# One core, a two-layer RWKV / attention decoder with 16 experts per layer: the list of tokens per expert is made by one-hot products, the router's parameters come a stage earlier, and the router's product stands on four column groups

## What is computed

```python
def hier_moe(x, w_grp, b_grp, w_exp, b_exp, w_gate, w_up, w_down):
    grp_logits = (t @ w_grp) + b_grp                 # 512 x 4
    grp = argmax(grp_logits); p_grp = softmax(grp_logits)[grp]
    exp_logits = (t @ w_exp) + b_exp                 # 512 x 4 x 4
    sel = exp_logits of the chosen group
    top_v, top_i = lax.top_k(sel, 2); top_w = softmax(top_v)
    gate = one_hot(grp) * within(top_i, top_w) * p_grp   # 512 x 16
    for e in range(16):                              # hidden width 512
        hdn = silu(t @ w_gate[e]) * (t @ w_up[e])
        y = y + gate[:, e:e + 1] * (hdn @ w_down[e])

h = x
for layer in (0, 1):
    h = h + (rwkv7_time_mix if layer == 0 else dilated_attention)(rmsnorm(h, norm_mix_g[layer]))
    h = h + hier_moe(rmsnorm(h, norm_ffn_g[layer]), ...)
return rmsnorm(h, final_norm_g)
```

## Time and profile before

| | us |
|---|---|
| median of three runs | 1850.54 |
| lowest, highest | 1848.89, 1855.57 |
| the profiled execution, its own time | 1855.97 |
| its span in the trace | 1854.3 |
| granted TensorE clock, mean | 0.882 of full speed |
| PE, DVE, ACT, POOL busy | 1457.0, 1029.9, 821.4, 269.7 |

### The profile page before, as it was taken

One profiled execution on the slowest core, in us unless ns is written; L12 is line 12 of the kernel. 1 busy time (PEld: TensorE's weight loads), 2 busy tenths in 40 slices (PEclk: granted clock), 3 DMA queues, 4 the chain that ended last, 5 costly groups with the idle time before them and its releaser, 6 DMA issues. The chain is left out here.

```text
span 1854.3 us, 28295 instructions
## 1 busy us (share of the span) xinstructions
PE 1457.0 (79%) x11205; PEld 1099.6 (59%) x11205; DVE 1029.9 (56%) x1191; ACT 821.4 (44%) x1169; POOL 269.7 (15%) x255
## 2 busy tenths in 40 slices
PE   3899986677715837999996499999985449999991
PEld 2273864566613316788775386777774337887771
DVE  4332446444455055888884524444445438888883
ACT  2223323344410025777774333334441327777761
POOL 1000017533231021010111200000001030111101
PEclk8598995899966968999998699999976769999995
DMA  4032200011160075999995422111200549999974
GB/s 143 2 139 87 91 1 0 22 27 26 26 266 36 14 272 186 393 393 391 393 391 188 155 91 68 46 46 46 69 0 1 195 148 377 393 391 392 391 296 159
DMA packets 162389, 313.02 MB, mean 169 GB/s; under 512 B 30256, under 2 KB 31536, under 8 KB 161520
## 3 DMA queue, kind: packets, MB, share of 16 engines
q1 hardware_dynamic: 149904, 265.36, 40.3%
q0 software_dynamic: 7488, 25.24, 3.7%
q10 hardware_dynamic: 4896, 20.97, 2.8%
HBM read 282.12 MB, written 29.43 MB: 168 GB/s over the span
## 5 line engine op out<-in xcount | busy, mean ns | idle before, releaser
L1158 DVE TENSOR_TENSOR moe_wlo<-moe_raw,moe_whi 128x2048 fp32r<-128x2048 f32 x192 | 436.7, 2290 | 88.2 <-ACT moe_whi L1154 88.0
L1154 ACT ACTIVATE moe_whi<-moe_raw 128x2048 fp32r<-128x2048 f32 x192 | 363.4, 1915 | 44.0 <-DMA moe_raw<-in_moe_w_down_dram 20.8
L1165 PE MATMUL all_bank<-moe_whi,moe_xhi 128*128 128x512 f32 x512 | 206.6, 403 | 4.1 <-DVE moe_xlo L1210 4.1
L1167 PE MATMUL all_bank<-moe_whi,moe_xlo 128*128 128x512 f32 x512 | 200.7, 392 | 0.0
L1166 PE MATMUL all_bank<-moe_wlo,moe_xhi 128*128 128x512 f32 x512 | 200.3, 391 | 0.0
L1165 PEld LDWEIGHTS all_bank<-moe_whi,moe_xhi 128*128 128x128 f32 x512 | 97.0, 189 | 23.5 <-DVE moe_xlo L1210 4.9
L1167 PEld LDWEIGHTS all_bank<-moe_whi,moe_xlo 128*128 128x128 f32 x512 | 96.6, 189 | 20.9
L1166 PEld LDWEIGHTS all_bank<-moe_wlo,moe_xhi 128*128 128x128 f32 x512 | 97.1, 190 | 18.3
L1165 PE MATMUL all_bank<-moe_whi,moe_hhi 128*128 128x512 f32 x256 | 102.8, 402 | 4.4 <-issue 4.4
L1166 PE MATMUL all_bank<-moe_wlo,moe_hhi 128*128 128x512 f32 x256 | 101.4, 396 | 0.0
L1167 PE MATMUL all_bank<-moe_whi,moe_hlo 128*128 128x512 f32 x256 | 101.3, 396 | 0.0
(11 more groups left out here) (366 smaller groups left out, 2963.9 us busy)
## 6 DMA issues: line engine op xcount, KB each, us to landing
moe_raw<-in_moe_w_gate_dram SPq DMA_DIRECT2D x64, 1024.0 KB, 12.4
moe_raw<-in_moe_w_up_dram SPq DMA_DIRECT2D x64, 1024.0 KB, 13.2
moe_raw<-in_moe_w_down_dram SPq DMA_DIRECT2D x64, 1024.0 KB, 12.0
out_dram<-moe_yo ACTq DMA_DIRECT2D x32, 512.0 KB, 6.3
attn_xhat<-in_w_kv_dram SPq DMA_DIRECT2D x10, 1024.0 KB, 5.0
attn_xhat<-in_attn_w_q_dram SPq DMA_DIRECT2D x6, 1024.0 KB, 4.9
all_h<-in_rwkv_w_v_dram SPq DMA_DIRECT2D x4, 1024.0 KB, 8.2
all_h<-in_rwkv_w_k_dram SPq DMA_DIRECT2D x4, 1024.0 KB, 6.3
```

The costliest lines, as they stand in the source:

```text
L1154: nc.scalar.activation(whi[slot % SPLITS][:, :], raw[slot % 6][:, :], ACT.Copy).then_inc(m["hi_ok"], 1)
L1158: nc.vector.tensor_tensor(wlo[slot % SPLITS][:, :], raw[slot % 6][:, :], whi[slot % SPLITS][:, :].bitcast(fp32), ALU.subtract).then_inc(m[ ...
L1165: nc.tensor.matmul(bank[b][:, :], hi[:, k0 + k, :], wh[:, k, :], start=begin and k == 0, stop=False)
L1167: ins = nc.tensor.matmul(bank[b][:, :], lo[:, k0 + k, :], wh[:, k, :], start=False, stop=end and k == 3)
```

## The change

Five things change.

*Parameters.* `router_load` issues the five router loads of an expert stage in the stage before it, on SP: behind the last load of the RWKV finish, and behind the sixth weight piece of attention. The tiles (`gain`, `wr`, `br`) live for the whole program. The final norm's gain row is loaded inside expert stage 1, behind its last weight pieces.

*Router product.* The router's weights are padded to 32 columns. Product kt writes output rows 32 (kt mod 4) to +31 of the bank, so that each of four column groups of the array sums two blocks. The four partial sums are added in the turn back: the copy is 128x512, and the four small products have the 128x20 matrix `quarters` (four stacked identities) as their moving operand.

*Table of tokens.* DVE compares the rank with a row 0..127 to give one-hot rows `hot` (128 x 4 x 128 for each choice), POOL multiplies `M1` and `M2` with the token numbers to `mtok`, and eight products `hot`ᵀ x `mtok` give the table of 128 places x 16 experts in a PSUM bank. The scattered writes, the zeroed DRAM table and the read back are gone. Columns for ranks of 128 and more are made only in the overflow path.

*Order on DVE.* The cast to `idx` comes first, then two of the four splits, the split of the first tokens, and the other two splits. Place, offsets and `pos`, which only the combine and the overflow test need, come behind these.

*Prologue.* POOL clears `wr`, makes a row of 128 numbers and `quarters`.

```diff
+def router_load(sp, g, io, layer):
+    rows = lambda x: io[x][layer].rearrange("(k p) n -> p k n", p=P)
+    sp.dma_start(g["gain"][:, :], io["norm_ffn_g"]...to_broadcast([P, D])).then_inc(g["moe_in"], 16)
+    sp.dma_start(g["wr"][:, :, 0:4], rows("moe_w_grp")).then_inc(g["moe_in"], 16)
+    sp.dma_start(g["wr"][:, :, 4:20], rows("moe_w_exp")).then_inc(g["moe_in"], 16)
+    sp.dma_start(g["br"][:, 0:4], ...); sp.dma_start(g["br"][:, 4:20], ...)
...
+        def one_hot(out, places, k):
+            return nc.vector.tensor_tensor(out, g["iota"]...to_broadcast([P, J, P]),
+                                           places[:, k, :]...to_broadcast([P, J, P]), ALU.is_equal)
+        def token_list(out, rows):
+            for k in range(2):
+                for j in range(J):
+                    ins = nc.tensor.matmul(out, rows[:, k, j, :], mtok[:, k, j, :], start=k == 0 and j == 0, stop=k == 1 and j == J - 1)
...
         @block.gpsimd
-            pool.wait_ge(pos_ok, 2)
-            pool.wait_ge(tok_zero, 16)
             for k in range(2):
-                for j in range(J):
-                    pool.indirect_dma_start(tok_dram, ...pos[:, k, j:j + 1]..., g["tokid"][:, j:j + 1], None)
-            pool.wait_ge(tok_st, 16 * 2 * J)
-            pool.dma_start(tokrow[:, :], tok_dram...)
+                nc.gpsimd.tensor_tensor(mtok[:, k, :, :], v64[1 + k]..., g["tokid"]..., ALU.mult).then_inc(mtok_ok, 1)
             pool.wait_ge(idx_ok, 1)
...
         @block.vector
-            dve.wait_ge(par_in, 80)
+            dve.wait_ge(par_in, PAR)
...
+                one_hot(hot[:, k, :, :], posf, k).then_inc(hot_ok, 1)
+            dve.wait_ge(idx_mm, 1)
+            V.tensor_copy(idx[:, 0:NE], bank[7][:, 0:NE]).then_inc(idx_ok, 1)
+            for k in range(2):
+                split_lo(dve, main, *piece(0, 0, k)[:2])
+            dve_tokens(dve, main, 0, 0)
+            for k in range(2, SPLITS):
+                split_lo(dve, main, *piece(0, 0, k)[:2])
...
         @block.tensor
-                last = nc.tensor.matmul(bank[0][0:NG + NE, :], wr[:, kt, :], xnT[:, kt, :], start=kt == 0, stop=kt == KT - 1)
+                c = 32 * (kt % 4)
+                last = nc.tensor.matmul(bank[0][c:c + 32, :], wr[:, kt, :], xnT[:, kt, :], start=kt < 4, stop=kt >= 4)
...
-                ins = nc.tensor.transpose(bank[1]..., lgT[:, P * j:P * j + P], g["ident"][0:NG + NE, 0:NG + NE])
+                ins = nc.tensor.matmul(bank[1]..., lgT[:, P * j:P * j + P], g["quarters"][:, :], start=True, stop=True)
...
-            pe.wait_ge(tok_in, 16)
-            nc.tensor.transpose(bank[2][:, 0:NE * J], tokrow[:, :], ...).then_inc(tok_tr, 1)
-            pe.wait_ge(idx_ok, 1)
+            pe.wait_ge(mtok_ok, 2)
+            pe.wait_ge(hot_ok, 2)
+            token_list(bank[7][:, 0:NE], hot).then_inc(idx_mm, 1)
...
 def final_norm(nc, io, g, out):
-            sp.dma_start(gb[:, :], io["final_norm_g"]...).then_inc(g_in, 16)
-            dve.wait_ge(g_in, 16)
+            dve.wait_ge(g["moe_in"], 176)
```

More of the change, by code:

```diff
@@ L101, in rwkv_project @@
         wlo = [s.sb(f"wlo{i}", [P, 4, 512], fp32r) for i in range(2)]
-        lh = s.sb("lora_hidden", [P, 2, T])
+        lh = g["gain"][:, :].rearrange("p (a b) -> p a b", a=2)
         parrow = s.sb("parrow", [P, P])
@@ L1080, in moe @@
         xnT = s.sb("xnT", [P, KT, T])
-        gb = s.sb("gb", [P, D])
+        gb, wr, br = g["gain"], g["wr"], g["br"]
         raw = [s.sb(f"raw{i}", [P, PIECE]) for i in range(6)]
@@ L1107, in moe @@
         wgt = s.sb("wgt", [P, 2, J])
-        zeros = s.sb("zeros", [NE * J, P])
-        tokrow = s.sb("tokrow", [NE * J, P])
+        place = s.sb("place", [P, 2, J])
+        mtok = s.sb("mtok", [P, 2, J, NE])
         idx = s.sb("idx", [P, NE * J], i32)
@@ L1128, in moe @@
         main, more = loop_sems(""), loop_sems("more_")
-        xn_dram, tok_dram, out_dram = io[f"xn_dram{layer}"], io[f"tok_dram{layer}"], io[f"out_dram{layer}"]
+        xn_dram, out_dram = io[f"xn_dram{layer}"], io[f"out_dram{layer}"]
         block = s.enter_context(nc.Block())
         xnT2 = xnT[:, :, :].rearrange("p a b -> p (a b)").rearrange("p (j d) -> p j d", j=J)
+        hot = yo[:, :].rearrange("p (k j r) -> p k j r", k=2, j=J)
+        late = xn[:, :, :].rearrange("p a b -> p (a b)").rearrange("p (b k j r) -> p b k j r", b=4, k=2, j=J)
+        par_in = g["moe_in"]
+        PAR = 80 * (layer + 1)
+        def one_hot(out, places, k):
+            return nc.vector.tensor_tensor(out, g["iota"][:, :].rearrange("p (x r) -> p x r", x=1).to_broadcast([P, J, P]),
+                                           places[:, k, :].rearrange("p (j x) -> p j x", x=1).to_broadcast([P, J, P]), ALU.is_equal)
+        def token_list(out, rows):
+            for k in range(2):
+                for j in range(J):
+                    ins = nc.tensor.matmul(out, rows[:, k, j, :], mtok[:, k, j, :], start=k == 0 and j == 0, stop=k == 1 and j == J - 1)
+            return ins
         def start(eng, m, names):
@@ L1478, in _ @@
             dve.wait_ge(rank_done, 1)
-            ch.link(V.tensor_copy(rank[:, 0, :], bank[1][:, 0:NE]))
+            ch.link(V.tensor_copy(rank[:, 0, :], bank[7][:, 64:64 + NE]))
+            V.tensor_copy(most_in, bank[7][:, 64 + NE:64 + 2 * NE])
             for j in range(1, J):
@@ L1489, in _ @@
                 tt(first_place[:, :, :], first_place[:, :, :], later[:, :, :], ALU.add)
-            tt(posf[:, :, :], posf[:, :, :], first_place[:, :, :], ALU.add)
-            V.tensor_copy(pos[:, :, :], posf[:, :, :]).then_inc(pos_ok, 1)
-            reduce(most[:, 0:1], bank[1][:, NE:2 * NE], ALU.max)
+            tt(place[:, :, :], posf[:, :, :], first_place[:, :, :], ALU.add)
+            V.tensor_copy(pos[:, :, :], place[:, :, :]).then_inc(pos_ok, 1)
+            reduce(most[:, 0:1], most_in, ALU.max)
             V.tensor_copy(mosti[:, :], most[:, 0:1]).then_inc(pos_ok, 1)
-            for k in range(SPLITS):
-                split_lo(dve, main, *piece(0, 0, k)[:2])
-            dve.wait_ge(tok_tr, 1)
-            V.tensor_copy(idx[:, 0:NE * J], bank[2][:, 0:NE * J]).then_inc(idx_ok, 1)
-            dve_tokens(dve, main, 0, 0)
             def round_(e, x):
@@ L1520, in _ @@
                 start(dve, more, ["split_ok", "xl_ok", "hid_ok", "hl_ok"])
+                dve.wait_ge(xn_st, 16)
+                for b in range(1, J):
+                    ch.link(V.tensor_scalar(later[:, :, :], posf[:, :, :], float(P * b), None, ALU.subtract))
+                    for k in range(2):
+                        one_hot(late[:, b, k, :, :], later, k).then_inc(late_hot, 1)
+                    dve.wait_ge(late_hot, 2 * b)
+                dve.wait_ge(late_mm, 1)
+                V.tensor_copy(idx[:, NE:NE * J], bank[7][:, NE:NE * J]).then_inc(idx_ok, 1)
                 def further_round(e, b, c):
@@ L1585, in _ @@
                 start(pe, more, ["piece_used", "xt_done", "ht_done"])
+                for b in range(1, J):
+                    pe.wait_ge(late_hot, 2 * b)
+                    ins = token_list(bank[7][:, NE * b:NE * b + NE], late[:, b, :, :, :])
+                ins.then_inc(late_mm, 1)
                 pe.wait_ge(main["y_ok"], 2 * NE + 1)
@@ L2014, in final_norm @@
     with Scope(nc, "final") as s:
-        gb = s.sb("gb", [P, D])
+        gb = g["gain"]
         ss, rstd = s.sb("ss", [P, J]), s.sb("rstd", [P, J])
-        g_in, rms, rstd_ok, done, stored = map(s.sem, ["g_in", "rms", "rstd_ok", "done", "stored"])
+        rms, rstd_ok, done, stored = map(s.sem, ["rms", "rstd_ok", "done", "stored"])
         block = s.enter_context(nc.Block())
@@ L2083, in _ @@
                 keep(g["upper"][:, :], 0.0, ALU.is_ge, -1, 1, -1)
+                ch.link(nc.gpsimd.tensor_copy(g["quarters"][:, :], g["ident"][:, 0:20]))
+                for c in range(32, P, 32):
+                    ch.link(nc.gpsimd.tensor_tensor(g["quarters"][:, :], g["quarters"][:, :], g["ident"][:, c:c + 20], ALU.add))
                 for rows, base in ((P, C), (C, 0)):
```

64 lines of the change are left out of this document (35 added, 29 removed).

## The result

The changed kernel takes 1803.83 us (median of four runs, 1803.32 to 1804.86) against 1850.86 us for the kernel before, run beside it on the same chip (four runs, 1848.89 to 1855.57). The ratio is 0.9743, 95% interval 0.9727 to 0.9758: 47.0 us less, where 44.0 were forecast (1806.5 us). The profiled execution took 1803.43 us, 52.5 less than the profiled one before.

What follows compares the result with a forecast made beforehand. The loop over experts was taken as full, so only the serial chain ahead of it, twice, could shrink: 22.1 and 21.9 us per stage, with 1.85 - 1.9 at the ends, make 44.0, so 1806.5 us; range 1793 to 1821.

Steps and rivals of the forecast that it cites:

- Parameters: Scaling ahead of the router: earlier loads end DVE's wait, gaining 5.17 and 4.30 us; moved loads cost nothing.
- Router: Router product before the first expert: four column groups run side by side, gaining 4.1 us per stage, bounds 0 and 4.1.
- rival A: Router product: column groups run in series, total gain only 35.8 us, time 1814.7; chance 0.13.
- The turn back: Turning router results back: four full float32 products cost 1.0 us more per stage, bounds 0.2 and 1.5.
- Table: Rank copy to end of cast: 7.4 us instead of 25.95, gaining 18.5 us in stage 0, 19.2 in stage 1.
- Held up by the splits: After the cast: POOL's column copy and indirect transfer wait for DVE's running splits, losing 3.1 us per stage.
- Rival B: After the cast: gather isn't held up by splits and small beside weights, 9.4 us more gain, 1797.1; chance 0.16.
- The gather beside the weights: First gather: freed buffers' 1 MB weight transfers run beside it, losing 1.6 us per stage, from 0 to 2.6.
- Ends: Program ends: final scaling no longer waits for its gain row, gain 1.85 us; longer prologue loses 1.9.
- rival D: Expert loop: PE clock stays at 1.2 GHz for rounds, making it slower, 1868.5 us with four; chance 0.04.
- Rival C: Expert loop: weight stream sets the stage's end and doesn't move with the first product, 1841.1 us; chance 0.04.
- The signs: Trace checks, including 14.4 us from cast to first product; wrong if the loop's length differed by over 2 us.

Runs made afterwards that it cites:

- e1: Changed kernel with the router's parameter loads back in their own expert stage and the gain row in the final norm; 1819.95 us, ratio 0.9799.
- e8: Changed kernel, but PE starts the router's sixteen passes only when all eight copies to xnT are done; one run, 1810.33 us.
- e4: Changed kernel with the place arithmetic moved back directly behind the cast to idx, ahead of the splits; 1796.59 us, ratio 0.9684.
- e7: Changed kernel, with the first freed weight buffer refilled only after the first gather has landed; 1796.65 us, ratio 0.9701.
- e11: Changed kernel with place arithmetic ahead of the splits and constant tables made on POOL beside the RWKV projections, not in the prologue; 1792.87 us, ratio 0.9682.
- e6: The changed kernel, unchanged, run again in a later go; 1802.05 us, ratio 0.9734.
- e10: Changed kernel with the old kernel's two token-table DRAM tensors declared again in their old places; 1806.17 us.
- e9: Kernel before, with the two token-table DRAM tensors declared behind all others; 1854.09 us.
- e12: Kernel before, with the weight buffers 2176 bytes further in each SBUF partition, where the changed kernel has them; 1851.73 us, ratio 0.9993.
- e2: Changed kernel with the router's eight products in series on the same 20 columns and the old turn back; 1814.1 us, ratio 0.9774.

## Why the prediction was right, step by step

The time fell by 47.0 us where 44.0 stood, and up to the first product the two stages gained 22.5 and 22.9 us where 22.1 and 21.9 were worked out for the whole stage.

- *Parameters*, 5.17 and 4.30: 5.18 and 4.31 in the trace, e1 takes them back. The moved loads cost nothing that shows: attention is 413.09 us against 412.78.
- *Router*, 4.1: 4.07 and 4.19. The row of quarters in the RWKV chunks was the right neighbour, and rival A falls with e8. The turn back cost 0.65 instead of 1.0: its four products, two passes each, take 1.07 us at a clock of 1.00, 0.27 a product, and the 0.45 came from a stretch at 0.50. The table's eight products ran at 0.50 and took 3.57 us, 0.45 each.
- *Table*, 18.5 and 19.2: 18.8 and 19.45 (the old table scatters by 1 us). The sum of the new chain was 7.4 us and is 7.16. POOL's products took 0.54 us for both, where up to 4.2 were allowed for, and end ahead of the rank copy.
- *Held up by the splits*, 3.1: 3.1, with the copy at 1.91 us and the transfer at 2.27. Rival B falls; e4 shows that it could be had by order alone.
- *The gather beside the weights* is the priced term that was most mis-sized: 1.6 us was put from 0 to 2.6, and it is 2.4 (5.75 against 3.33), as e7 shows.
- *Ends*: 1.85 and -2.07 against 1.85 and -1.9. In time the second is unproven (e11).
- *Not in the sum, gains*: the turns of `xn` became 0.6 and 0.9 us shorter, and the loop lost its slow tail, 1.6 and 3.0 us with what follows. The prediction read the stream as even with PE at 398 GB/s, from one stretch early in the loop; three to five rounds at its end took 18.7 us at 392. The loop was put at nothing for want of that view, and it is the largest miss. One view of the round times of the kernel before would have shown it. That the change would move the weight buffers was in the diff as well.
- *Not in the sum, a loss*: from the first product to the second turn of gathered tokens there are 8.0 to 8.2 us in the changed kernel (six stages of three traces, its own, e6's and e10's) and 6.9 to 8.4, mean 7.5, in eight stages of the kernel before and its two variants e9 and e12. In the two traces below the first products run at the lower clock for longer after the change:

```profile
684.00:689.00 5.00, 5.00 (x12) 3.92 (x13) 4.90 (x6) 0.21 (x1) 0.00 (x0) 0.50 0.68 194
689.00:694.00 5.00, 5.00 (x27) 4.18 (x26) 1.63 (x11) 1.95 (x2) 0.18 (x1) 0.98 0.85 331
```

Those are twelve passes in the 5 us behind the first product, clock 0.50; the kernel before has 16, clock 0.71:

```profile
707.40:712.40 5.00, 5.00 (x16) 4.06 (x17) 0.00 (x0) 0.38 (x1) 0.02 (x1) 0.71 0.36 105
```

That is rival D in small, about 0.7 us per stage; at 689 to 694 the clock is 0.98. e2, with the router as before, has 7.94 and 8.07, so the shorter router doesn't cause it. e4, e7 and e11, whose gather comes sooner, have 7.2 to 7.9, but so has e8 (7.35 and 7.27), whose gather doesn't; what causes it is open.

- *Rival C* fell with the first product: the loop moved with it.
- *The signs.* All that were named for the inside of the stages came, the way from the cast to the first product with 15.25 us for 14.4. One sign of being wrong came too: a loop that differs by more than 2 us. In stage 1 the stretch from the first product to the final norm is 3.0 us shorter. It points at the weight stream, not at the chain.

The terms as measured make 45.4 us to the first products, -0.2 at the ends and 4.6 in the loops, 49.8 in all, against 47.0 by the medians (45 to 50.5 by the interval). Of the 44.0 that were forecast, the chain came out at 45.2 with the ends; that the median came out so near is in part luck, as 4.6 us of the trace's gain were in no term and 2.8 of the trace's 49.8 are not in the medians. The rest of the 52.5 between the two profiles is the RWKV part's scatter of 3.1 less attention's 0.3.

## What to carry to other kernels

Ahead of a loop that is full, count the serial chain by its end and price each link by the nearest row: all priced links but one were right to 0.4 us here. When a long wait disappears, look at what is queued right behind it; here the new order put DVE's longest instructions onto POOL's most urgent ones, and moving some lines gave 10 us back. Look at every round of a loop before calling it steady, and when a change touches the allocations, ask which transfers' addresses it moves (here that showed in the rounds, and in the time by 3.5 us at most).

## What the hardware showed beyond expectation

- Four column groups of TensorE on the same 128 rows: 16 passes of 512 columns in 1.92 us, 3.7 times as fast as the 7.03 us in series (e8, e2).
- The 1 MB weight transfers ran at 392 GB/s into buffers at byte 73,856 of a partition and at 400 to 410, about the 403 that a round asks for, into buffers 2176 bytes further; a gate piece landed after 14.2 us in the kernel before (900 to 920 us), after 8.9 in the changed one (880 to 900 us) and after 9.6 in e12 (900 to 920 us).
- POOL's copy of 128 numbers takes 0.19 us alone, 1.13 us in the loop of the changed kernel and 1.91 when it starts 0.4 us behind the start of a split (668.88 against 668.47); beside a split it ends with that split, to 0.1 us.
- A gather of 128 rows is seen by PE 3.3 us behind the end of its issue alone and 5.75 us beside two pieces of weights (e7 and the changed kernel: 3.23 and 5.75).
